# Query and key projection in high and low halves, key chunks first, with the low halves and their sums on GpSimd

## The reference, cut to what matters

```python
proj = modulate(layer_norm(stream), shift, scale) @ w_in
qk_pre, v, o_pre, g, f_in = jnp.split(proj, SPLITS, axis=-1)
qk = jax.nn.silu(conv_fn(qk_pre, conv_w, conv_b))   # 3x3 depthwise on the latent grid, 1-D on the context
q, k = jnp.split(qk, 2, axis=-1)
...
h_fwd, st_fwd = mlstm_chunkwise(q, k, v, log_i[0], log_f[0], states[0])
h_bwd, st_bwd = mlstm_chunkwise(rev(q), rev(k), rev(v), rev(log_i[1]), rev(log_f[1]), states[1])
```

## Time and profile before

| what | us |
|---|---|
| median of 3 runs (lowest, highest) | 1789.82 (1787.89, 1794.53) |
| span of the profiled execution, first to last instruction | 1786.4 |
| TensorE busy in it | 1707.3 |
| VectorE, ScalarE, GpSimd busy | 1144.2, 794.2, 540.3 |
| mean granted TensorE clock, share of full speed | 0.993 |

### The profile page before, as it was taken

One profiled execution on the slowest core, in us unless ns is written; L12 is line 12 of the kernel. 1 busy time (PEld: TensorE's weight loads), 2 busy tenths in 40 slices (PEclk: granted clock), 3 DMA queues, 4 the chain that ended last, 5 costly groups with the idle time before them and its releaser, 6 DMA issues.

```text
span 1786.4 us, 32548 instructions
## 1 busy us (share of the span) xinstructions
PE 1707.3 (96%) x7475; PEld 1237.2 (69%) x7476; DVE 1144.2 (64%) x1692; ACT 794.2 (44%) x1098; POOL 540.3 (30%) x578
## 2 busy tenths in 40 slices
PE   7999999998889999899999998999999999999997
PEld 1545454446854477788888777888888887888874
DVE  4773775403877869667538788654768588275647
ACT  0211112122231032557547788554767577265534
POOL 2000000004832320134334354333444344333442
PEclk9999999999999999999999999999999999999999
DMA  9752000011334241768959899866789789587765
GB/s 380 270 225 96 1 0 0 1 37 42 107 143 182 106 165 54 296 206 301 286 101 363 288 353 334 307 158 220 231 308 333 193 305 371 120 291 210 223 204 202
DMA packets 95503, 357.79 MB, mean 200 GB/s; under 512 B 19389, under 2 KB 19550, under 8 KB 86757
## 3 DMA queue, kind: packets, MB, share of 16 engines
q1 hardware_dynamic: 65298, 288.49, 42.2%
q0 software_dynamic: 30160, 68.76, 17.3%
q10 hardware_dynamic: 4, 0.02, 0.0%
HBM read 330.96 MB, written 70.62 MB: 225 GB/s over the span
## 4 chain that ended last, share of the span: by engine, by line
PE 72%; DMA 14%; DVE 6%; issue 3%; ACT 2%; SPq 1%; POOL 1%; ACTq 1%; DVEq 0%; POOLq 0%
DMA sum_rows<-arena,idxs 11%; PE psum L1356 8%; PE psum L1358 8%; PE psum L1357 8%; PE psum L1082 7%; PE psum L1187 5%; PE psum L1091 4%; PE psum L1343 4%; PE psum L1380 3%; PE psum L1378 3%; PE psum L1379 3%; PE psum L1029 3%; PE psum L1122 3%; DMA raw_weights<-in_w_gu 2%; DVE arena L1711 1%
## 5 line engine op out<-in xcount | busy, mean ns | idle before, releaser
L1972 DVE TENSOR_TENSOR split_weights<-raw_weights,split_weights (+1 forms) x366 | 429.3, 1221 | 56.4 <-ACT split_weights L698 39.2
L698 ACT ACTIVATE split_weights<-raw_weights (+1 forms) x366 | 364.6, 1059 | 47.6 <-issue 24.1
L698 ACT ACTIVATE arena<-psum 128x1024 f32<-128x1024 f32 (+6 forms) x187 | 154.4, 830 | 493.3 <-PE psum L1082 107.1
L1356 PE MATMUL psum<-split_weights,split_rows 128*128 (+1 forms) x832 | 335.8, 404 | 2.4 <-DVE split_rows L1961 2.4
L1358 PE MATMUL psum<-split_weights,split_rows 128*128 (+1 forms) x832 | 326.8, 393 | 0.0
L1357 PE MATMUL psum<-split_weights,split_rows 128*128 (+1 forms) x832 | 325.3, 391 | 0.0
L654 POOL DMA_INDIRECT sum_rows<-arena,idxs x102 | 175.4, 1720 | 230.6 <-DMA sum_rows<-arena,idxs 191.3
L1358 PEld LDWEIGHTS psum<-split_weights,split_rows 128*128 128x128 f32 x832 | 156.9, 189 | 34.7
L640 POOL COPY idxg<-idxT 128x1 uint32 (+1 forms) x107 | 72.4, 676 | 358.7 <-DVE split_rows L1961 286.8
L1356 PEld LDWEIGHTS psum<-split_weights,split_rows 128*128 128x128 f32 x832 | 157.8, 190 | 31.6 <-DVE split_rows L1961 2.6
L1357 PEld LDWEIGHTS psum<-split_weights,split_rows 128*128 128x128 f32 x832 | 157.5, 189 | 30.1
(11 more groups left out here) (312 smaller groups left out, 2314.3 us busy)
## 6 DMA issues: line engine op xcount, KB each, us to landing
raw_weights<-in_w_gu SPq DMA_DIRECT2D x62, 2048.0 KB
raw_weights<-in_w_dn SPq DMA_DIRECT2D x62, 1024.0 KB
arena<-in_w_ada SPq DMA_DIRECT2D x12, 2048.0 KB, 8.8
arena<-in_toks SPq DMA_DIRECT2D x18, 512.0 KB, 9.2
arena<-job_rows SPq DMA_DIRECT2D x16, 512.0 KB, 3.7
arena<-in_w_vog SPq DMA_DIRECT2D x1, 4160.0 KB, 14.4
arena<-in_w_qk SPq DMA_DIRECT2D x1, 4096.0 KB, 17.2
arena<-in_w_out SPq DMA_DIRECT2D x2, 2048.0 KB, 9.8
```

The costliest lines, as they stand in the source:

```text
L698: return act.activation(o, i, ACT.Copy)
L1356: mm(bank(3 + p), xk, part(par, 0, 512 * k), start=(k == 0), stop=False)
L1972: tt(cols(wsplit, (1 - par) * (2 * WE) + (WE + 1024 * c), 1024), cols(raw, (1 - par) * WE + 1024 * c, 1024), high, ALU.subtract).then_inc( ...
```

## The change

Each operand of the query and key projection is written as a high half (rounded to the reduced-precision float type that TensorE takes in one pass, `F32R`) and a low half (the rest). The product is high x high + high x low + low x high, three matmuls for each k instead of one in float32.

- ScalarE makes the high halves: `u_high` of the latent columns, eight instructions of 128x1024 behind the evacuations of the Fourier input; `uc_high` of the context, two; the weights, one 128x1024 for each chunk (`weight_high`), one chunk ahead.
- GpSimd makes the low halves (`less`), that of `uT` in place, when the Fourier input projection is done. After the projection it adds the halves up to `uT` again (`both`), which values and gates read.
- Weights come in eight DMAs of 512 KB into two buffers, in a layout made on the host.
- Key chunks come first. `cacc` has two buffers. The context's gate part comes second of three.
- Two tables in the constants (`C_REV`, `C_SEL`), which nothing reads, are gone: 1111 columns instead of 2263.

```diff
-        QKJOBS = [(c, part) for c in range(8) for part in range(3 if c >= 4 else 2)]
+        QKORDER = (4, 5, 6, 7, 0, 1, 2, 3)
+        QKJOBS = [(i, c, part) for i, c in enumerate(QKORDER) for part in range(3 if c >= 4 else 2)]
...
+            def load_qk(i):
+                if i >= 2:
+                    sp.wait_ge(S("front_mm"), QK_DONE_0 + QKENDS[i - 2])
+                sp.dma_start(wq_raw[i % 2], a["w_qk"][P * QKORDER[i]:P * QKORDER[i] + P, :]).then_inc(S(f"wqk_in{i % 2}"), 16)
...
+            def less(o, x, high):
+                pool.tensor_tensor(o, x, high.bitcast(F32), ALU.subtract).then_inc(S("front_low"), 1)
+
+            def both(k, n0, n1, high):
+                pool.tensor_tensor(uT[:, k, n0:n1], u_low[:, k, n0:n1].bitcast(F32), high.bitcast(F32), ALU.add).then_inc(S("front_back"), 1)
...
+            pool.wait_ge(S("front_mm"), 8)
+            for k in range(8):
+                pool.wait_ge(S("front_high"), HIGH_X + k + 1)
+                less(u_low[:, k, CTX:], uT[:, k, CTX:], u_high[:, k])
+            weight_low(0)
+            for h in range(2):
+                pool.wait_ge(S("front_high"), HIGH_C + h + 1)
+                less(u_low[:, 4 * h:4 * h + 4, 0:CTX], uT[:, 4 * h:4 * h + 4, 0:CTX], uc_high[:, 4 * h:4 * h + 4])
+            for i in range(1, 5):
+                weight_low(i)
+            pool.wait_ge(S("front_mm"), QK_DONE_0 + QKENDS[3])
+            for h in range(2):
+                k = slice(4 * h, 4 * h + 4)
+                both(k, 0, CTX, uc_high[:, k])
+            for i in range(5, 8):
+                weight_low(i)
+            pool.wait_ge(S("front_mm"), QK_DONE_0 + QKENDS[6])
...
+            for part in range(2):
+                pool.wait_ge(S("front_mm"), QK_DONE_0 + QKENDS[7] - 1 + part)
+                for h in range(4):
+                    k = slice(2 * h, 2 * h + 2)
+                    both(k, CTX + 512 * part, CTX + 512 * part + 512, u_high[:, k, 512 * part:512 * part + 512])
...
+            for i in range(9):
+                for q, (chunk, c, part) in enumerate(QKJOBS):
+                    if chunk != i:
+                        continue
+                    act.wait_ge(S("front_mm"), QK_DONE_0 + q + 1)
+                    if part == 0 and i >= 2:
+                        act.wait_ge(S("front_dve"), CONV_DONE_0 + i - 1)
+                    if part == 2 and i >= 1:
+                        act.wait_ge(S("front_dve"), CONV_DONE_0 + i)
...
+                    if part == 0 and i + 1 < 8:
+                        weight_high(i + 1)
...
+            act.wait_ge(S("front_back"), BACK_X + 8)
             for t in range(NTC):
                 values(t)
...
                 for k in range(8):
-                    ins = mm(bank(q % 4)[:, 0:n], wqk[:, k, P * c:P * c + P], uT[:, k, o:o + n], start=(k == 0), stop=(k == 7))
+                    wh, wl = (w[i % 2][:, P * k:P * k + P] for w in (wq_high, wq_low))
+                    uh = u_high[:, k, o - CTX:o - CTX + n] if part < 2 else uc_high[:, k]
+                    mm(bank(q % 4)[:, 0:n], wh, uh, start=(k == 0), stop=False)
+                    mm(bank(q % 4)[:, 0:n], wh, u_low[:, k, o:o + n], start=False, stop=False)
+                    ins = mm(bank(q % 4)[:, 0:n], wl, uh, start=False, stop=(k == 7))
...
+            pe.wait_ge(S("front_back"), 2)
             values(0)
             values(1)
...
             for r, (o0, o1, w) in enumerate(GATEPARTS):
+                pe.wait_ge(S("front_back"), BACK_X + (4, 4, 8)[r])
...
-                if c >= 1:
-                    dve.wait_ge(S("silu_done"), c)
+                if i >= 2:
+                    dve.wait_ge(S("silu_done"), i - 1)
+                acc = cacc[i % 2]
```

More of the change, by code:

```diff
@@ L58 @@
 F32R = mybir.dt.float32r
-C_ID, C_REV, C_MF, C_MB, C_ONE, C_LT, C_IOTA, C_SEL = (i * P for i in range(8))
-C_HALF = C_SEL + 8 * P
+C_ID, C_MF, C_MB, C_ONE, C_LT, C_IOTA = (i * P for i in range(6))
+C_HALF = C_IOTA + P
 C_TOK = C_HALF + 16
@@ L80, in constant_tiles @@
     c[:, C_IOTA:C_IOTA + P] = p[None, :]
-    for r in range(8):
-        c[r, C_SEL + r * P:C_SEL + (r + 1) * P] = 1
     c[:, C_HALF:C_HALF + 16] = -0.5
@@ L124, in build @@
         arena = sb("arena", ARENA)
+        extra_base = (nc.sbuf_base + 31) // 32 * 32
+        extra = sb("extra", 2048)
         def at(o, n):
@@ L418, in _ @@
             sp.dma_start(wvog, drows(a["w_vog"], 0, 1040)).then_inc(S("wvog_in"), 16)
+            for i in range(2, 8):
+                load_qk(i)
             sp.wait_ge(S("rows_exp"), 5)
@@ L717, in _ @@
                 copy(fT[:, c, 512 * h:512 * h + 512], bank(4 + i % 2)).then_inc(S("front_evac"), 1)
+                if i == 0:
+                    act.wait_ge(S("uT_act"), 16)
+                    act.wait_ge(S("uT_dve"), 8)
+                copy(u_high[:, i], uT[:, i, CTX:]).then_inc(S("front_high"), 1)
                 if i == 6:
@@ L725, in _, with weight_high @@
                 copy(G[0][:, c], bank(2 * (c % 2)).rearrange("p (s n) -> p s n", s=4)).then_inc(S("ab_act"), 1)
+            def weight_high(i):
+                act.wait_ge(S(f"wqk_in{i % 2}"), 16 * (i // 2 + 1))
+                copy(wq_high[i % 2], wq_raw[i % 2]).then_inc(S("front_high"), 1)
             act.wait_ge(S("front_mm"), AB_DONE_0 + 9)
@@ L733, in _ @@
                     copy(qtmp[:, g, 0:w], bank((4 if c % 2 else 0) + 2 * g + 1)[:, 0:w]).then_inc(S("front_evac"), 1)
+                if c == 0:
+                    act.wait_ge(S("mrow_out"), 32)
+                    weight_high(0)
+                if c < 2:
+                    act.wait_ge(S("folded"), 2)
+                    copy(uc_high[:, 4 * c:4 * c + 4], uT[:, 4 * c:4 * c + 4, 0:CTX]).then_inc(S("front_high"), 1)
             act.wait_ge(S("cbuf_zero"), 2)
             act.wait_ge(S("small_in"), 48)
[L737 to L750, removed]
-                if c >= 1:
-                    act.wait_ge(S("front_dve"), CONV_DONE_0 + c)
-                    x = c - 1
-                    act.activation(qkT[:, x, :], cacc.rearrange("p r c -> p (r c)"), ACT.Silu, bias=convb[:, x:x + 1]).then_inc(S("silu_done"), 1)
@@ new lines, in _ @@
+            for i in range(9):
[7 more added lines that the diff above has]
+                        act.wait_ge(S("front_dve"), CONV_DONE_0 + i)
+                    if part < 2:
+                        copy(cbuf[i % 2][:, 1 + 8 * part:9 + 8 * part, 1:65], bank(q % 4).rearrange("p (r c) -> p r c", r=8)).then_inc(S("front_evac"), 1)
+                    else:
+                        copy(cbufc[:, 1:257], bank(q % 4)[:, 0:256]).then_inc(S("front_evac"), 1)
+                    if part == 0 and i + 1 < 8:
+                        weight_high(i + 1)
+                if i >= 1:
+                    act.wait_ge(S("front_dve"), CONV_DONE_0 + i)
+                    x = QKORDER[i - 1]
+                    if i == 5:
+                        act.wait_ge(S("front_back"), 2)
+                    act.activation(qkT[:, x, :], cacc[(i - 1) % 2].rearrange("p r c -> p (r c)"), ACT.Silu, bias=convb[:, x:x + 1]).then_inc(S("silu_done"), 1)
@@ L1075, in _ @@
             pe.wait_ge(S("front_dve"), QTMP_USED_0 + 8)
-            pe.wait_ge(S("wqk_in"), 16)
-            for q, (c, part) in enumerate(QKJOBS):
+            for q, (i, c, part) in enumerate(QKJOBS):
+                if part == 0:
+                    pe.wait_ge(S("front_low"), weight_split(i))
+                if q == 2:
+                    pe.wait_ge(S("front_low"), HIGH_C + 2)
                 if q >= 4:
```

65 lines of the change are left out of this document (38 added, 27 removed).

## The result

| | before | changed |
|---|---|---|
| median, lowest to highest (us, 6 runs each) | 1788.72, 1786.81 to 1794.53 | 1797.19, 1795.84 to 1798.96 |
| ratio to before, 95% interval | 1 | 1.0043, 1.0033 to 1.0053 |
| span of the profiled execution | 1786.4 | 1793.7 |
| mean granted TensorE clock | 0.993 | 0.983 |

The forecast was 1797 us. The change costs 8.5 us, within the 0.5% that was called no change, though the interval says that it is slower.

What follows compares the result with a forecast made beforehand. TensorE bound the kernel, with about 14.8 us of slack on VectorE. GpSimd's turns would spend the 23.5 us that TensorE saves, a net +7.1: 1786.4 + 7.1 + 3.4 = 1797 us, range 1765 to 1812.

Steps and rivals of the forecast that it cites:

- Turns in whole instructions: Folds and convolution: GpSimd and VectorE instructions with two SBUF inputs run one at a time; likeliest case, chance 0.70.
- theory A: Forecast for the added copies: GpSimd takes the shared path only for two SBUF inputs, so total 1797 to 1798 us.
- Folds +14.0: VectorE's folds before the projection: GpSimd's lows of x come in between them and delay everything up to the projection 14.0 us.
- Start of the projection 165.2: Query and key projection starts at 152.6 - 1.4 + 14.0 = 165.2 us.
- 2.2 us for each turn: Each GpSimd operation holds VectorE 2.2 us; 16 in the convolution stage make 35.2 us.
- Third value tile 314.6: TensorE's third value tile waits for an evacuation behind the last Silu: 314.6 us, where it was 307.45, so +7.1.
- Constants -1.4: Constants shrink from 1131.5 to 555.5 KB, so the first matmuls wait less: -1.4 us for the whole program.
- 3.4 us around the span: Median of the runs 1789.8 against a profiled span of 1786.4; the 3.4 us between is taken as lying around the span.
- folds spared: Rival: only the folds escape GpSimd's turns, +7.1 - 14.0, 1783 us; chance 0.05, split between faster and same.
- no turns: Rival: no turns in projection and folds, TensorE binds, 24.9 us less, 1765 us; chance 0.13.
- Slow lows: Rival: GpSimd is slow at writing rounded halves, 3.5 us more a low, +42, 1839 us; chance 0.08.
- VectorE keeps its turn: Rival: GpSimd starves until a chunk ends, lows and sums come late, 1790 to 1805 us; chance 0.04.

Runs made afterwards that it cites:

- experiment 3: Changed kernel with a second GpSimd sum of 1024 elements, two SBUF inputs, before each of the eight x sums: 1813.86 us.
- experiment 1: Changed kernel with GpSimd's eight lows of x waiting until VectorE's last fold is done: 1781.78 us, ratio to before 0.9954.
- 7: experiment 1 with the eight x sums also moved from GpSimd to VectorE: 1773.54 us, ratio 0.9916.
- 8: 7 with the weight lows of chunks 2 to 7 and both context sums also moved to VectorE: 1769.55 us, ratio 0.9891.
- experiments 2: Changed kernel with a GpSimd memset of 1024 elements added before each of the eight x sums: 1797.87 us.
- experiment 6: Changed kernel with a GpSimd copy of 1024 elements from SBUF added before each of the eight x sums: 1805.46 us.
- 5: Changed kernel with TensorE doing 80 unused 128x128 multiplications while it waits for the third fold: 1797.82 us.
- experiment 4: Changed kernel with one product instead of three in the query and key projection, both low-half products left out: 1790.2 us.

## Why the prediction was right

By its own steps:

- **Turns in whole instructions** were the cause. Seen directly in both places (folds of 2.1 to 2.7, convolution instructions of 3.3), doubled for the sums by experiment 3, taken out by experiment 1 in the folds and by 7 and 8 in the projection. The Trainium skill's rule ("SBUF — State Buffer", "Who interferes with whom") names any GpSimd instruction that reads SBUF, and not one that only writes; experiments 2 (nothing for a memset between two-input instructions) and 6 (0.64 for a copy) agree with both halves. My own theory A in experiment 6 was narrower than that rule and than the chip.
- **Folds +14.0**: measured +13.8 (20.4 from the first fold of the chain to the products of the last, before 6.6).
- **Start of the projection 165.2**: measured 167.32. The missing 2.1 is a term that the sum did not have: TensorE, idle for 10.99, went on at a lower granted clock, and the two groups of products behind the fourth fold took 3.78 and 1.52 where they had taken 2.05 and 1.04. Experiments 1 and 5 show it.
- **First chunk 14.5**: measured 14.48. **Products 0.23 apart**: 0.23. Those of 256 columns start 0.12 apart, in place of the 0.129 assumed.
- **2.2 us for each turn**: the term that was mis-sized. The chain's rows give 2.0 (a held instruction is followed by the next 3.29 to 3.35 later, a free one 1.32), though GpSimd's own 2.37 was right: more of its start goes into the turn than the 0.15 that I took from the earlier trace rows. The number of turns, 16 in the stage, was right. 16 x 0.2 = 3.2 of the 3.5 by which the stage is shorter (144.1, forecast 147.6).
- **Third value tile 314.6**: measured 313.07, +2.1 for the clock and -3.5 for the stage. The gates before it ended at 309.1 rather than near 305: TensorE left the projection at 278.0 and not 275.5, and the prediction's own 275.5 with the two value tiles and gates of the earlier trace rows (30.9) gives 306.4, not 305. They were hidden nevertheless. The gap is 3.94 and not 7.
- **Constants -1.4**: the first matmuls' last group starts at 34.24, before 35.59.
- **3.4 us around the span**: the profiled execution had 2.1, the rest was how that execution differed from the median. The 1789.8 that the forecast started from was the median of three executions; that of six is 1788.7. The forecast's +7.1 to the third value tile was +5.6 here; 5.9 stand at 545.54; the rest up to the 8.5 of the medians lies in the long expert stretch, whose length differs by up to 4.4 between profiled executions of these kernels. So of the agreement to 0.2 us at least 2 is chance.

Three slips in the working, none of which moved the forecast. The lower bound for the small job (2.6 instead of 3.1) is 2 us less in all four, not 3.6; measured is 24 x 0.12 = 2.9. The folds take up to 0.70 each, not 0.61 or less. And the 0.18 for faster counts all of *folds spared* (0.05), whose 1783 lies among the times called the same.

The rivals: *no turns* and *folds spared* fall with the rows above. *Slow lows*: 2.37 with rounded output and for the weight low as well; the type costs GpSimd nothing. *VectorE keeps its turn*: each GpSimd operation got in behind at most one VectorE instruction. That the projection was no longer TensorE's was shown by experiment 4. The balance at the third value tile: -1.4 constants, +13.8 folds, +2.2 clock, +5.8 for the stage up to the last Silu (144.1 in place of 138.3: 32 of turns against 26 saved by the earlier first chunk, the second accumulator and faster products), -14.8 of slack that VectorE had: +5.6. What TensorE saves is real: in experiment 8 the third value tile starts at 284.62, 22.8 before the 307.45 of the kernel before, 2.5 of it before the projection began and 20.3 behind that, with the wait of 2.47 in it (forecast for the products 23.5). In the changed kernel GpSimd's turns had spent it.

## What to carry to other kernels

GpSimd is no spare engine beside a VectorE whose instructions have two SBUF inputs: what it reads there is charged to VectorE, 2.0 us for 1024 elements which VectorE does itself in 1.15. Put GpSimd's work beside stretches in which VectorE reads PSUM or waits (experiment 1: one wait, 15 us), and give the rest to VectorE. When an engine is relieved, look for the next shortest slack behind it before counting the gain: here 23.5 us on TensorE met 14.8 us of slack on VectorE, and a TensorE that had been idle for 5.5 us or more came back at a lower clock here.

## What the hardware showed that I had not expected

- After idleness of 5.5 to 11 us, work on TensorE was slower: 16 products of 128 columns 3.79 instead of 2.05 (idle 10.99), 16 matmuls of 512 columns 10.16 (idle 5.51) and 10.21 (idle 10.03) instead of 7.03. After 3.9 to 4.4 us it was 7.13 to 8.83, and the idle time just before does not tell which: 3.94 gave 7.13 in the changed kernel, 3.92 gave 8.83 in experiment 5. The mean clock from 118 to 182 us was 0.84 in the changed kernel.
- A VectorE instruction with one SBUF input is held too: the convolution's first took 2.92 beside a sum, alone 0.75.
- A GpSimd copy of 1024 elements (1.09) holds VectorE 0.64, a sum (2.37) holds it 2.0, a memset (0.96) doesn't hold it; all three for a VectorE instruction with two SBUF inputs.
- GpSimd and VectorE write rounded halves as fast as plain float32: for 1024 elements GpSimd took 2.37 for a low and 2.39 for the shorter of its two context sums, VectorE 1.22 for a low and for a sum (in a row they start 1.15 apart).
